# The last two expert items summed inside the core, and the bias sums between the last weight chunks, in a retention, sparse attention and mixture-of-experts layer

## What is computed

```
h2 = rms_norm(x, norm2_g) * (1 + sc2) + sh2
top_vals, top_idx = top_k(h2 @ router_w + router_b, 4);  gates = softmax(top_vals)
for expert e, for its tokens:  gu = xb @ w_gu[e] + b_gu[e]
    ys = ((clip(up) + 1) * glu(gate)) @ w_down[e] + b_down[e]
y = sum over a token's 4 experts of gate * ys
out = rms_norm(x + g2 * y, final_g)
```

## Time and profile before

| what | us |
|---|---|
| median of 3 runs | 1465.04 (1462.0 to 1465.07) |
| the profiled execution | 1465.49 |
| its span, first to last instruction | 1463.6 |
| outside the span | 1.9 |
| PE busy | 1328.7 (91%) |
| DVE, ACT, POOL busy | 839.1, 727.7, 361.0 |
| moved by DMA | 475.90 MB, mean 325 GB/s |

### The profile page before, as it was taken

How to read it: one execution, slowest core, us unless ns; L and a number is a source line. 1 busy time by engine, 2 the same in 40 slices (tenths; PEclk the granted TensorE clock), 3 DMA queues, 4 the chain that set the end, 5 groups by cost and what they waited for, 6 DMA issues and landing times.

```text
span 1463.6 us, 17803 instructions
## 1 busy us (share of the span) xinstructions
PE 1328.7 (91%) x6418; PEld 866.9 (59%) x6423; DVE 839.1 (57%) x947; ACT 727.7 (50%) x940; POOL 361.0 (25%) x318
## 2 busy tenths in 40 slices
PE   4999999999999897998979898989899897998986
PEld 1657885558757374775554675737477465756432
DVE  0576775446947273775463774727378446758234
ACT  3542325546736354665372763636466536637222
POOL 2000020112133232321423332323233141413220
PEclk9999999998999999999999999999999999999998
DMA  9656530055989999999999999999999999999996
GB/s 343 201 166 230 204 131 15 9 195 183 341 329 403 400 371 403 381 396 383 383 392 386 383 390 390 390 385 364 399 370 402 384 373 383 392 383 381 383 392 217
DMA packets 95129, 475.90 MB, mean 325 GB/s; under 512 B 23687, under 2 KB 33903, under 8 KB 42817
## 3 DMA queue, kind: packets, MB, share of 16 engines
q1 hardware_dynamic: 82656, 451.39, 78.4%
q0 software_dynamic: 12304, 23.22, 5.9%
q10 hardware_dynamic: 80, 0.13, 0.0%
HBM read 468.16 MB, written 23.09 MB: 336 GB/s over the span
## 4 chain that ended last, share of the span: by engine, by line
PE 69%; DMA 14%; ACT 9%; DVE 4%; SPq 2%; issue 2%; DVEq 0%; ACTq 0%
DMA ring<-in_w_down 13%; PE bank L1727 9%; PE bank L1730 9%; PE bank L1734 9%; PE bank L1776 6%; PE bank L1761 4%; PE bank L1511 4%; ACT e_hi L906 3%; PE bank L1323 3%; PE bank L1806 3%; PE bank L1325 3%; PE bank L1324 3%; ACT area L909 3%; PE bank L1798 3%; PE bank L1799 2%; DVE e_lo L1984 2%
## 5 line engine op out<-in xcount | busy, mean ns | idle before, releaser
L1984 DVE TENSOR_TENSOR e_lo<-ring,e_hi 128x2048 fp32r<-128x2048 f32 x216 | 485.0, 2287 | 269.4 <-ACT e_hi L906 269.2
L906 ACT ACTIVATE e_hi<-ring 128x2048 fp32r<-128x2048 f32 x216 | 409.6, 1919 | 317.7 <-DMA ring<-in_w_down 254.7
L1761 PE MATMUL bank<-ring,area 128*64 128x512 f32 x896 | 204.0, 602 | 37.8 <-DMA ring<-in_w_gu 37.8
L1727 PE MATMUL bank<-e_hi,x_hi 128*128 128x512 f32 x576 | 227.2, 394 | 0.0
L1730 PE MATMUL bank<-e_hi,x_lo 128*128 128x512 f32 x576 | 224.7, 390 | 0.0
L837 POOL COPY future<-routes 128x1 int32 (+1 forms) x31 | 113.9, 3674 | 395.6 <-DVE area L2320 274.8
L1798 PE MATMUL bank<-e_hi,act_hi 128*128 128x512 f32 x288 | 121.3, 421 | 50.1 <-ACT e_hi L906 50.0
L1761 PEld LDWEIGHTS bank<-ring,area 128*64 128x64 f32 x896 | 60.3, 137 | 171.6 <-issue 101.2
L1734 PE MATMUL bank<-e_lo,x_hi 128*128 128x512 f32 x576 | 154.2, 390 | 0.0
L1727 PEld LDWEIGHTS bank<-e_hi,x_hi 128*128 128x128 f32 x576 | 108.2, 188 | 26.2 <-issue 4.1
L1734 PEld LDWEIGHTS bank<-e_lo,x_hi 128*128 128x128 f32 x576 | 108.2, 188 | 22.7
(11 more groups left out here) (296 smaller groups left out, 1734.3 us busy)
## 6 DMA issues: line engine op xcount, KB each, us to landing
ring<-in_w_gu SPq DMA_DIRECT2D x256, 1024.0 KB, 9.7
ring<-in_w_down SPq DMA_DIRECT2D x128, 1024.0 KB, 10.8
ring<-in_ada_w SPq DMA_DIRECT2D x24, 1024.0 KB, 9.2
ring<-in_w_in SPq DMA_DIRECT2D x9, 1024.0 KB, 7.9
ring<-in_w_o SPq DMA_DIRECT2D x4, 1024.0 KB, 7.7
xs<-in_x SPq DMA_DIRECT2D x4, 512.0 KB, 5.2
ring<-in_w_in SPq DMA_DIRECT2D x8, 256.0 KB, 5.3
xn_rows<-area POOLq DMA_DIRECT2D x4, 512.0 KB, 5.1
```

What stands on the lines that cost most here:

```text
L906: return nc.scalar.activation(dst, src, ACT.Copy, scale=scale)
L1727: pe.matmul(bank[b][:], x_hi[:, c, :], hi, start=False, stop=False)
L1761: mm = pe.matmul(bank[g // 2][half, :], xgT[:, c, 0:NARROW], w[:, 512 * g:512 * g + 512], start=False, stop=(c == GU - 1))
L1984: tt(e_lo[c % PARTS][:], raw(period.raw_slot(c)), e_hi[:, c % PARTS, :].bitcast(F32), ALU.subtract).then_inc(lo_ready, 1)
```

## The change

Item 30 is no longer scattered: it is treated like item 31, and the one-hot products of both work on two row halves. The half of the output columns that lies in PSUM rows 64 to 127 stays there: DVE scales the whole bank in one instruction (`tail_out`) with a copy of the gate and of g2 laid out in the same way, and `tail_sum` multiplies rows 0 to 63 for the first 512 columns and rows 64 to 127 for the others. The ACT copies of the upper rows go for items 30 and 31. `b_rows` now lies where `x_lo` was (free after item 29's gate-up), and its loads are issued after item 29's down chunks, ahead of item 31's 8 gate-up chunks. `down_narrow` of item 31 calls `beside_last` after each chunk: the gate transpose after the first, the bias and item-30 sums of token group 0 after the second, of group 1 after the third. Those of group 2 follow the fourth chunk, ahead of the branch; those of group 3 come after item 31's sums of groups 0 to 2. `all_scattered` now waits for items 0 to 29 only, and for the gates of item 31.

```diff
+        one_hots = [view(11264, T, P), view(7696, T, P)]
+        tail_rows = [view(11776, 512), view(8208, 512)]
+        b_rows = nc.alloc_sbuf_tensor_at("b_rows", [P, D], F32, offset=-(-nc.sbuf_base // 32) * 32)
-        b_rows = ring[:, 4 * SLOT:4 * SLOT + D]
...
@@ SP
+                if i == E - 2:
+                    sp.wait_ge(chunk_used, Later(ORDER.rindex("H")).at(GU))
+                    sp.wait_ge(b_rows_stored, 16)
+                    load_b_rows()
             closing(E, e_before)
-            raw_free(Later(E), DN)
-            sp.wait_ge(b_rows_stored, 16)
...
@@ POOL
-            add_rows(E - 1, slice(E - 2, E - 1), ys, early=True)
-            pool.wait_ge(scattered, (E - 1) * 16)
+            pool.wait_ge(gate_in, E * 16)
+            pool.wait_ge(scattered, (E - 2) * 16)
...
@@ ACT
-                if not wide(i - 1):
+                if not wide(i - 1) and i < E - 1:
-            a.wait_ge(chunk_used, MAIN_CHUNKS)
-            copy(last_upper[0:NARROW, :], bank[0][NARROW:P, :]).then_inc(upper_moved, 1)
...
@@ TensorE
-            down_narrow(Later(E), 0, bank[0], last_actT, gate_turn)
+            def tail_sum(item, t):
+                for half in range(2):
+                    rows = slice(NARROW * half, NARROW * half + NARROW)
+                    mm = pe.matmul(bank[SUM_BANKS[t] + half][:], one_hots[item][rows, t, :],
+                                   tail_rows[item][rows, :], start=False, stop=(item == 1))
+                return mm
+            def first_sums(t):
+                bias_sum(t, 0)
+                bias_sum(t, 1)
+                tail_sum(0, t)
+            def beside_last(n):
+                if n == 0:
+                    gate_turn()
+                if n == 1:
+                    pe.wait_ge(gate_t_ready, 1)
+                    pe.wait_ge(b_rows_in, 64)
+                    pe.wait_ge(y_ready, E)
+                    first_sums(0)
+                if n == 2:
+                    first_sums(1)
+            down_narrow(Later(E), 0, bank[0], last_actT, beside_last)
+            first_sums(2)
             with pe.If(n_over > 0):
...
             pe.wait_ge(rows_left, 1)
-            for t in range(T - 1):
-                last_rows(t)
-            bias_sum(T - 1, 0)
-            bias_sum(T - 1, 1)
-            last_rows(T - 1)
+            for t in range(T):
+                if t == T - 1:
+                    first_sums(t)
+                tail_sum(1, t).then_inc(sum_full, 1)
...
@@ DVE
+            def tail_places(item, p):
+                for half in range(2):
+                    rows = slice(NARROW * half, NARROW * half + NARROW)
+                    done(nc.vector.tensor_copy(last_token_of[rows, 4:5], tok_i[0:NARROW, p:p + 1]))
                 for t in range(T):
                     done(ts(last_token_of[:, t:t + 1], last_token_of[:, 4:5], -float(P * t), None, ALU.add))
                 for t in range(T):
+                    done(ts(one_hots[item][:, t, :], iota_p, last_token_of[:, t:t + 1], None, ALU.is_equal))
+            def tail_gate(i, column):
+                v.wait_ge(gate_in, i * 16)
+                done(nc.vector.tensor_copy(column[NARROW:P, :], column[0:NARROW, :]))
+            def tail_out(item, i, sums, column):
+                v.wait_ge(chunk_used, Later(i).at(CHUNKS) if i < E else MAIN_CHUNKS)
+                stt(out=tail_rows[item], in0=sums, scalar=column, in1=g2_halves, op0=ALU.mult,
+                    op1=ALU.mult).then_inc(y_ready, 1)
...
+            v.wait_ge(act_ready, E)
+            for half in range(2):
+                rows = slice(NARROW * half, NARROW * half + NARROW)
+                done(nc.vector.tensor_copy(g2_halves[rows, :], g2_row[rows, 512 * half:512 * half + 512]))
+            tail_places(0, E - 2)
+            tail_gate(E - 1, gate)
+            tail_out(0, E - 1, bank[4][:], gate)
             gate_sums()
-            last_one_hot()
-            last_rows_out()
+            tail_places(1, E - 1)
+            tail_gate(E, gate_last)
+            tail_out(1, E, bank[0][:], gate_last)
```

More of the change, by code:

```diff
@@ L102 @@
 NARROW = 64
-assert len(ORDER) == E and ORDER[:2] == "HH" and ORDER[-1] == "L"
+assert len(ORDER) == E and ORDER[:2] == "HH" and ORDER[-2:] == "LL"
 N_WIDE = ORDER.count("H")
@@ L235, in build @@
         upper = view(15360, 512)
-        last_upper = view(13824, 512)
+        g2_halves = upper
         actT = view(5632, 4, P)
@@ L497, in half_cols, with scattered_by @@
             return slice((n % 2) * 512, (n % 2) * 512 + 512)
+        def scattered_by(i):
+            return i - 1 if isinstance(i, int) and i <= E else i - 3
         def bias_of(i):
@@ L647, in _, with load_b_rows @@
             opening(0, 0)
+            def load_b_rows():
+                for t in range(T):
+                    sp.dma_start(b_rows[32 * t:32 * t + 32, :].rearrange("e (g n) -> e g n", g=4),
+                                 b_rows_dram.rearrange("g e n -> e g n")).then_inc(b_rows_in, 16)
             e_before, e = 0, 1
@@ L672, in _ @@
                 sp.wait_ge(lo_ready, splits_before(Later(ITEMS).at(0)))
-            for t in range(T):
-                sp.dma_start(b_rows[32 * t:32 * t + 32, :].rearrange("e (g n) -> e g n", g=4),
-                             b_rows_dram.rearrange("g e n -> e g n")).then_inc(b_rows_in, 16)
+                sp.wait_ge(xlo_ready, 2 * wides_before(ITEMS) + 2)
+                sp.wait_ge(chunk_used, Later(ITEMS).at(0))
+                load_b_rows()
+                sp.wait_ge(tail_restored, 1)
             sp.wait_ge(all_scattered, 1)
@@ L829, in load_gates, with add_rows @@
                 pool.sem_clear(sidx_ready)
-            def add_rows(i, before, rows, early=False):
-                if not early:
-                    pool.wait_ge(y_ready, i + 1)
+            def add_rows(i, before, rows, tail):
+                pool.wait_ge(y_ready, i + 1)
                 if i is not 1:
-                    pool.wait_ge(scattered, (i - 1) * 16)
+                    pool.wait_ge(scattered, (i - 1 - tail) * 16)
                 pool.tensor_copy(aidx.bitcast(I32), tok_i[:, before]).then_inc(aidx_ready, 1)
-                if early:
-                    pool.wait_ge(y_ready, i + 1)
                 pool.wait_ge(aidx_ready, 1)
@@ L845, in add_rows, with store @@
                 pool.sem_clear(aidx_ready)
-            def store(i, before):
+            def store(i, before, tail):
                 load_gates(before, gate)
-                add_rows(i, before, ys)
+                add_rows(i, before, ys, tail)
             def opening(i):
@@ L855, in opening, with steady @@
                 bring(i, slice(i + 2, i + 3))
-            def steady(i):
+            def steady(i, tail=0):
                 if i is 1:
                     bring(1, slice(3, 4))
-                    store(1, slice(0, 1))
+                    store(1, slice(0, 1), 0)
                     return
@@ L863, in steady @@
                 bring(i, bass.ds(after, 1))
-                store(i, bass.ds(before, 1))
+                store(i, bass.ds(before, 1), tail)
             def closing(i):
-                store(i, slice(i - 1, i))
-                pool.wait_ge(scattered, i * 16)
+                store(i, slice(i - 1, i), 2)
+                pool.wait_ge(scattered, (i - 2) * 16)
             opening(0)
@@ L889, in _ @@
                 with pool.Fori(E + 1, ITEMS) as i:
-                    steady(i)
+                    steady(i, 2)
                 closing(ITEMS)
@@ L1779, in down_narrow @@
                     mm.then_inc(chunk_used, 1)
-                    if between is not None and n == 2:
-                        between()
+                    if between is not None:
+                        between(n)
             def down(period, c0, between=None):
@@ L1848, in steady, with last_act_turn @@
                 down(period, GU)
-            def last_act_turn():
+            def last_act_turn(n):
+                if n != 2:
+                    return
                 pe.wait_ge(act_ready, E)
@@ L1879, in _, with bias_sum @@
             last_steady()
-            down_narrow(Later(E), 0, bank[0], last_actT, gate_turn)
+            def bias_sum(t, half):
+                rows = slice(32 * t, 32 * t + 32)
+                return pe.matmul(bank[SUM_BANKS[t] + half][:], gate_t[rows, :],
+                                 b_rows[rows, half * 512:half * 512 + 512], start=True, stop=False)
+            def tail_sum(item, t):
+                for half in range(2):
+                    rows = slice(NARROW * half, NARROW * half + NARROW)
+                    mm = pe.matmul(bank[SUM_BANKS[t] + half][:], one_hots[item][rows, t, :], tail_rows[item][rows, :],
+                                   start=False, stop=(item == 1))
+                return mm
[15 more added lines that the diff above has]
+            first_sums(2)
             with pe.If(n_over > 0):
+                pe.wait_ge(tail_kept, 1)
+                for t in range(T - 1):
```

(22 more changed lines are left out.)

14 lines of the change are left out of this document (5 added, 9 removed).

## The result

The changed kernel takes 1468.08 us (median of 7 runs, 1466.85 to 1470.12), the kernel before 1462.47 (7 runs, 1460.12 to 1465.07) beside it: ratio 1.004, 95% interval 1.0028 to 1.0052. It is 5.6 us slower.

A forecast was written before the change was run, and what follows sets the result against it. The saturated weight stream was taken as the bound. Moved loads, chunks and sums put the first add at 1450.5, 1.0 us later, giving 1466.0 us by the median; range 1462.9 to 1469.2, the forecast's own 1464.8 to 1467.6.

The forecast's parts named there:

- The bound: Until its last chunk the weight stream sets the time, at about 420 GB/s; bytes added ahead of that chunk cost time.
- first rival: The stream hides b_rows without delaying item 31: first add 1448.0, 1.5 us faster, 1464.0; chance 0.20.
- Part 1: b_rows loads moved into the stream ahead of item 31's chunks: 2.8 us, between bounds of 1.3 and 7.
- upper bound of 7 us: Most the moved loads could cost: stretch 1433 to 1443 took 10 us where 420 GB/s would have taken 3.
- second rival: b_rows holds back weights 5 us or more, deciding from a price of 4.7 us: 1468 to 1470; chance 0.11.
- The sums on TensorE: Item 31's chunks with sums between them, 11.65 us, then 3.93 to the first add at 1450.5.
- The third rival: Half-row passes run one after the other, 0.86 us more per `tail_sum`, 3.4 in all: 1469.4; chance 0.07.
- The branch: Branch over code of further items, 3.69 us from 1444.7, ends by 1448.4 hidden under TensorE's products.
- The clock: Full clock through the sums, gaining the 1.7 us lost at half clock from 1445.6 to 1449.1.
- The loads of `sum_rows`: Issued at about 1428 behind the weights, landed by 1446, off the path; chunks 2 and 3 have 2.4 and 4.8 us spare.
- The sum: First add at 1450.5 against 1449.47, 1.0 us later, so 1466.5 for the profiled execution, 1466.0 by the median.
- the wide range: 1462.9 to 1469.2 us, taking in the first rival with the runs' spread and most of the second and third.

The follow-up runs named there:

- e4: Kernel before with only the four b_rows loads moved ahead of item 31's gate-up chunks, all sums left behind the last chunk: 1466.49 us, ratio 1.0031.
- e10: e2 plus 512 KB of another tensor at the same place, in four loads of 32 partitions, rows of 4 KB: 1466.76 us in a single execution.
- e7: Kernel before, unchanged, traced a second time: 1460.69 us.
- e3: Changed kernel with its sums in blocks, bias products after item 31's second chunk and item 30's half-row products after the fourth: 1464.59 us, ratio 1.0014.
- e2: Changed kernel with one b_rows load instead of four, ACT copying the rows to the other three groups of 32 partitions: 1462.45 us, ratio 1.0005.
- e6: Changed kernel with one b_rows load, three ACT copies, and the sums in blocks: 1458.84 us, ratio 0.997 to the kernel before.

## Why the prediction was right or wrong, point by point

- **The bound.** The saturated stream is what the change hurt: right. That b_rows could not hide in it was right, too (first rival, 0.20: D would have stayed at 61).
- **The price of the moved loads: the step that failed.** Part 1 took 2.8 us, "what the same loads cost the weights beside them". They cost 6.2 (D 67.3 against 61.1). The row chosen was taken where few weights were left: 65 packets of 8 KB started beside b_rows there, and 232 in the full stream. Each was slowed alike (0.52 and 0.51 us instead of 0.31), so the harm was of the same kind and there was more to harm; e4's T shows the harm at the end again, as 2.3. The upper bound of 7 us, from ten microseconds at 124 GB/s, was the better guide: 244 GB/s for ten microseconds, and the second rival, "the moved loads cost the stream double", with its point of 4.7 us, is what happened. I gave it 0.11. I had put the low rate of the earlier trace rows down to engines without work; part of it was slowed packets.
- **The Trainium skill on it.** The Trainium skill, "SBUF — State Buffer", section "Door 1: The DMA port swizzle", says that bandwidth depends on how many ports the partitions reach, and that 32 partitions reach half. The trace agrees with the direction. The size differs: the estimate from the rule alone was 2.6 us for these loads, and the runs show 6.2 (and 6.6 for e10, 1.3 to 1.9 for the same bytes over 128 partitions), since the weights beside them are held up too (0.51 us a packet instead of 0.31). The measurement decides.
- **The sums on TensorE.** From chunk 1's start to the first add I had 15.58 us (11.65 + 3.93); measured 1452.35 - 1436.79 = 15.56. Chunk 1.87, bias 1.91, half rows 1.06 against 1.91, 1.91 and 1.05. The half rows run side by side (four passes in 1.06). The third rival, in series, is wrong.
- **The branch** took 3.54 us from 1446.5, ended at 1450.0, and the next sums began at 1450.24 behind the others: hidden, as said. The DVE instruction too.
- **The clock** was full through the sums. But the credit of 1.7 us for it was taken against one execution in which it happened to fall. Against the second execution of the kernel before, T is 20.5 against 20.3: no gain at all. The reason given for the fall, that TensorE had been idle ahead of it, is not borne out: it was about as idle in the second execution, and the clock stayed full (e7).
- **The loads of `sum_rows`** went out at 1430.56 and were off the path; they did not hold up the last chunks.
- **The sum.** Forecast +1.0 us against the profiled execution. Add 3.4 for the loads and 1.8 for the clock: 6.2, as the table has it.
- **How much of the nearness was luck.** The forecast of 1466.0 us stood on the median of 3 runs, 1465.04, for the kernel before; the seven runs beside the changed kernel gave 1462.47. On that, the forecast's +1.0 us would have been 1463.5, and the measured difference is 5.6. The measured 1468.08 lies outside the forecast's own 1464.8 to 1467.6, and inside the wide range of 1462.9 to 1469.2 only because that took in most of the second and third rivals.
- **What the working priced rightly but never named.** `first_sums` splits the bias products by group, so three row groups no longer run side by side, and it changes the form more often. That costs 4.3 us of T (e3). T is 18.0 in e4, where the loads are moved and the sums stand as before, 20.5 in the changed kernel and 16.2 in blocks. So sums in pieces cost 2.5 us, which used up the 2.3 that the freed end of the stream gave, and sums in blocks gain 1.8.

## What to carry to other kernels

A transfer to 32 partitions put into a saturated stream cost five times its bytes here (6.2 us against 1.3 at 420 GB/s), because it slows what moves beside it: load one copy and copy it on an idle engine (e2, e6), or look for a layout over all partitions. Price an insertion by a row where the queues are full, not by the harm it does where few transfers are left. Filling gaps of TensorE with pieces of a block was no gain where the block ran on several row groups at once; move the block whole. And one trace can hold an accident: compare distances between fixed points, not absolute times.

## What the runs showed of the hardware that I had not expected

- 512 KB to the same place in a full stream: 1.3 and 1.9 us over 128 partitions, 6.2 and 6.6 in quarters of 32.
- Pieces of 1 KB were not dearer than rows of 4 KB (1.3 against 1.9 us).
- While such loads ran, 16 busy DMA engines moved 232 to 252 GB/s instead of some 420, and an 8 KB packet of the weights took 0.49 to 0.53 us instead of 0.31.
